# Twelve-stage transformer kernel: in the first two attentions the output projection of the first token tile is issued behind the last six units; sparse attention's output projection takes its k tiles in another order

## What is computed

```python
na0:  neighbourhood attention, 16 heads of 64, position bias     (touched)
ffn0: silu(h @ Wg) * (h @ Wu) @ Wd, inner width 2816
dil0: dilated attention, 16 heads, three projections per head    (touched)
ffn1, ffn2
rwrt: two recurrent mixers side by side, then @ ev_w_out
xa0:  attention over a memory of 256 tokens, 4 heads
ffn3, ffn4
dsa:  sparse attention (top 64 of the keys for each token) for 8 heads,
      beside a short convolution over 512 channels;
      concat([o, conv]) @ od_w_out                               (touched)
xa1:  attention over the memory again (mem_norm @ wk, @ wv)      (its memory load is touched)
ffn5
```

## Time and profile before

| | |
|---|---|
| time of three runs | 2300.5, 2303.89, 2302.1 us; median 2302.1 us |
| profiled execution | 2304.5 us, its span 2302.7 us |
| busy | TensorE 92%, weight loads 85%, VectorE 62%, ScalarE 41% |
| TensorE's granted clock, mean | 0.947 of 2.4 GHz |

### The profile page before, as it was taken

One profiled execution on the slowest core, in us unless ns is written; L12 is line 12 of the kernel. 1 busy time (PEld: TensorE's weight loads), 2 busy tenths in 40 slices (PEclk: granted clock), 3 DMA queues, 4 the chain that ended last, 5 costly groups with the idle time before them and its releaser, 6 DMA issues.

```text
span 2302.7 us, 37011 instructions
## 1 busy us (share of the span) xinstructions
PE 2117.8 (92%) x14998; PEld 1948.3 (85%) x14998; DVE 1427.3 (62%) x1925; ACT 935.2 (41%) x1225; POOL 27.4 (1%) x46
## 2 busy tenths in 40 slices
PE   7989999999999999999955988999999996689998
PEld 6769989998879989998944977899899895588997
DVE  5747746665647756765677546576577455565773
ACT  4534434344444434444311324444444342444442
POOL 0000000000000000000000000000000000000000
PEclk9989999999999999999976978899999997898999
DMA  7325554443415554555520024255455551142553
GB/s 279 130 82 183 193 199 170 151 147 114 162 47 184 195 196 152 195 192 184 199 76 9 1 80 149 94 189 193 158 188 188 202 182 73 51 162 89 192 192 110
DMA packets 49789, 341.47 MB, mean 148 GB/s; under 512 B 5776, under 2 KB 6544, under 8 KB 9616
## 3 DMA queue, kind: packets, MB, share of 16 engines
q1 hardware_dynamic: 45216, 321.21, 38.6%
q10 hardware_dynamic: 4464, 18.68, 2.2%
HBM read 338.82 MB, written 1.05 MB: 148 GB/s over the span
## 4 chain that ended last, share of the span: by engine, by line
PE 81%; DVE 13%; ACT 3%; issue 2%; DMA 0%; POOL 0%; DVEq 0%; ACTq 0%; SPq 0%; POOLq 0%
PE pj L226 14%; PE pj L227 14%; PE pj L228 14%; PE acc L232 7%; PE acc L234 7%; PE acc L233 7%; DVE wlo L302 2%; PE pj L560 2%; PE acc L628 2%; PE pj L232 2%; PE pj L234 2%; PE pj L233 2%; PE pj L566 1%; ACT whi L295 1%; PE acc L616 1%
## 5 line engine op out<-in xcount | busy, mean ns | idle before, releaser
L302 DVE TENSOR_TENSOR wlo<-raw,whi 128x2048 fp32r<-128x2048 f32 x288 | 659.8, 2291 | 346.7 <-ACT whi L295 345.8
L226 PE MATMUL pj<-xh,whi 128*128 128x256 f32 x2704 | 771.1, 285 | 18.1 <-DVE wlo L312 13.2
L227 PE MATMUL pj<-xl,whi 128*128 128x256 f32 x2704 | 767.8, 284 | 0.0
L228 PE MATMUL pj<-xh,wlo 128*128 128x256 f32 x2704 | 767.7, 284 | 0.0
L295 ACT ACTIVATE whi<-raw 128x2048 fp32r<-128x2048 f32 x299 | 569.6, 1910 | 475.2 <-PE acc L234 240.8
L226 PEld LDWEIGHTS pj<-xh,whi 128*128 128x128 f32 x2704 | 521.9, 193 | 21.2 <-issue 15.7
L227 PEld LDWEIGHTS pj<-xl,whi 128*128 128x128 f32 x2704 | 522.0, 193 | 0.0
L228 PEld LDWEIGHTS pj<-xh,wlo 128*128 128x128 f32 x2704 | 521.8, 193 | 0.0
L232 PE MATMUL acc<-whi,AR 128*128 128x512 f32 x688 | 275.6, 401 | 9.5 <-DVE AR L1875 4.4
L233 PE MATMUL acc<-whi,AR 128*128 128x512 f32 x688 | 274.3, 399 | 0.0
L234 PE MATMUL acc<-wlo,AR 128*128 128x512 f32 x688 | 274.1, 398 | 0.0
(11 more groups left out here) (351 smaller groups left out, 2421.4 us busy)
## 6 DMA issues: line engine op xcount, KB each, us to landing
raw<-in_wstream SPq DMA_DIRECT2D x302, 1024.0 KB, 4.8
F<-in_gains ACTq DMA_DIRECT2D x12, 512.0 KB, 5.4
F<-in_rpb ACTq DMA_DIRECT2D x3, 1024.0 KB, 4.8
F<-in_memtok ACTq DMA_DIRECT2D x2, 1024.0 KB, 4.8
F<-in_memin ACTq DMA_DIRECT2D x2, 1024.0 KB, 6.9
F<-in_small ACTq DMA_DIRECT2D x1, 1536.0 KB, 10.6
F<-in_xin SPq DMA_DIRECT2D x2, 512.0 KB, 6.5
xt<-in_xtok SPq DMA_DIRECT2D x1, 1024.0 KB, 11.9
```

Source lines behind the costliest of these rows:

```text
L226: nc.tensor.matmul(o, wh, k_hi, start=first, stop=False, skip_group_check=True)
L227: nc.tensor.matmul(o, wh, k_lo, start=False, stop=False, skip_group_check=True)
L228: return nc.tensor.matmul(o, wl, k_hi, start=False, stop=last, skip_group_check=True)
L302: nc.vector.tensor_tensor(wlo[:, gs, :], raw[:, gs, :], whi[:, gs, :].bitcast(F32), ALU.subtract).then_inc(w_lo, 1)
```

## The change

`na0` and `dil0`: for i = 10 to 15 `fill(i)` ends in `first_half(i - 10)`, which issues the six 512-column matmuls of the first token tile (both column halves) for k tile i - 10, into `pj[0]` and `pj[1]`. They take the place of the filler matmuls of i = 12 to 15. `out_pe` leaves those products out of its first three chunks and does the rest: 12 matmuls in each of these chunks, 24 in the last. `post_act` and `post_dve` read the first token tile from `pj[0]`, `pj[1]`.

`dsa`: the weights' rows and the k tiles are taken in the order 4, 5, 6, 7, 0, 1, 2, 3, so the convolution's tiles come first; `out_pe` no longer waits for all eight tiles; the `UV` product goes behind the first chunk and into `pj[0]`, `pj[1]`. ACT rounds the convolution's tiles and issues the memory's loads ahead of the attention, and squares the memory right behind it; the memory's transposed copy gets another place in SBUF for this stage.

```diff
@@ -407,23 +407,27 @@
             nc.vector.tensor_scalar(ss[:, 8:10], ss[:, 4:6], 1.0 / D, EPS, ALU.mult, ALU.add)\
                 .then_inc(sg(tag, "mv"), 1)
-        def post_act(act, w, tag):
+        def out_banks(kind):
+
+            return [pj[0], pj[1], acc[2], acc[3]] if kind in ("na", "dil") else acc
+
+        def post_act(act, w, tag, ob):
             for b in range(4):
                 if b < 3:
                     act.wait_ge(*at(tag, "ob", b + 1))
                 else:
                     act.wait_ge(w_used, w.g + 1)
-                nc.scalar.activation(JUNK[:, b * 512:(b + 1) * 512], acc[b][:, :], ACT.Square, accum_out=ss[:, b:b + 1])\
+                nc.scalar.activation(JUNK[:, b * 512:(b + 1) * 512], ob[b][:, :], ACT.Square, accum_out=ss[:, b:b + 1])\
                     .then_inc(sg(tag, "sq"), 1)
             act_phase(act, w, 1)
-        def post_dve(dve, w, tag, half, nxt):
+        def post_dve(dve, w, tag, half, nxt, ob):
             tmp = [Sb[:, 0, :], Sb[:, 1, :], PTb[:, 0, :], PTb[:, 1, :]]
             def scaled(b):
                 dve.wait_ge(*at(tag, "sq", b + 1))
-                link(dve, nc.vector.scalar_tensor_tensor(tmp[b], acc[b][:, :], half * D ** 0.5,
+                link(dve, nc.vector.scalar_tensor_tensor(tmp[b], ob[b][:, :], half * D ** 0.5,
                                                          GB[:, (b % 2) * 512:(b % 2 + 1) * 512], ALU.mult, ALU.mult))
             def mean(t):
@@ -472,7 +476,8 @@
             for _ in range({3: 2, 4: 2, 5: 0}[n]):
                 nc.tensor.matmul(mb[:, T:2 * T], ident, cst[:, 0:T], start=True, stop=True)
-        def out_pe(pe, w, nk, lo_at, tag, ready, nxt, beside=lambda pe, c: None, fill=keep_busy, kt0=0):
+        def out_pe(pe, w, nk, lo_at, tag, ready, nxt, beside=lambda pe, c: None, fill=keep_busy, kt0=0,
+                   ob=acc, early=0):
             post = tag + "post"
             def last_chunk(g):
@@ -483,7 +488,7 @@
                     t, h = divmod(b, 2)
                     for kk in range(2):
                         wk = slice(kk * D + h * 512, kk * D + (h + 1) * 512)
-                        x = mm3t(acc[b][:, :], whi[:, gs, wk], wlo[:, gs, wk], AR[:, k0 + kk, t * P:(t + 1) * P],
+                        x = mm3t(ob[b][:, :], whi[:, gs, wk], wlo[:, gs, wk], AR[:, k0 + kk, t * P:(t + 1) * P],
                                  AR[:, lo_at + k0 + kk, t * P:(t + 1) * P], False, kk == 1)
                     if b == 3:
                         x.then_inc(w_used, 1)
@@ -509,12 +514,12 @@
                 pe.wait_ge(w_lo, g + 1)
                 for kk in range(2):
                     pe.wait_ge(*at(tag, ready, c * 2 + kk + 1))
-                    for b in range(4):
+                    for b in range(2 if c < early else 0, 4):
                         t, h = divmod(b, 2)
                         tt = slice(t * P, (t + 1) * P)
                         kt = (2 * c + kk + kt0) % nk
                         wk = slice(kk * D + h * 512, kk * D + (h + 1) * 512)
-                        x = mm3t(acc[b][:, :], whi[:, gs, wk], wlo[:, gs, wk], AR[:, kt, tt],
+                        x = mm3t(ob[b][:, :], whi[:, gs, wk], wlo[:, gs, wk], AR[:, kt, tt],
                                  AR[:, lo_at + kt, tt], c == 0 and kk == 0, False)
                 x.then_inc(w_used, 1)
                 beside(pe, c)
@@ -806,7 +811,8 @@
         mem_hi, mem_lo = AR[:, 16:24, :], AR[:, 24:32, :]
-        mem_raw = F0[:, 32 * T:40 * T].rearrange("p (k t) -> p k t", t=T)
+        raw_at = {mt_: F0[:, a:a + 8 * T].rearrange("p (k t) -> p k t", t=T)
+                  for mt_, a in (("s6m", 32 * T), ("s10m", 8984))}
         mem_tok = F0[:, 24 * T:32 * T].rearrange("p (t n) -> p t n", n=D)
         mem_rs = mn[:, 0:2]
@@ -837,14 +843,14 @@
             return fill
         def mem_act(act, mt, c):
-            if c == 0:
+            if c == (-1 if mt == "s10m" else 0):
                 act.wait_ge(*at(mt, "ld", 32))
                 for t in range(2):
                     nc.scalar.activation(JUNK[:, t * D:(t + 1) * D], mem_tok[:, t, :], ACT.Square,
                                          accum_out=mn[:, 2 + t:3 + t]).then_inc(sg(mt, "sq"), 1)
             if c == 1:
                 for k in range(KT):
-                    nc.scalar.activation(mem_hi[:, k, :], mem_raw[:, k, :], ACT.Copy, scale=v("mem_g", k))\
+                    nc.scalar.activation(mem_hi[:, k, :], raw_at[mt][:, k, :], ACT.Copy, scale=v("mem_g", k))\
                         .then_inc(sg(mt, "hi"), 1)
         def mem_dve(dve, mt, c):
...
@@ -983,13 +989,23 @@
                             w.g += 1
                             w.p += 1
                         done[0] += 1
-                    if i >= 3 * UP:
-                        for _ in range(3 if na else 5):
-                            nc.tensor.matmul(pj[0][:, 0:T], ident, cst[:, 0:T], start=True, stop=True)
+                    if i >= 10:
+                        first_half(i - 10)
+
+                def first_half(kt):
+
+                    c, kk = divmod(kt, 2)
+                    gs = (w.g + c) % 3
+                    pe.wait_ge(w_lo, w.g + c + 1)
+                    pe.wait_ge(*at(tag, "od", kt + 1))
+                    for h in range(2):
+                        wk = slice(kk * D + h * 512, kk * D + (h + 1) * 512)
+                        mm3t(pj[h][:, :], whi[:, gs, wk], wlo[:, gs, wk], AR[:, kt, 0:P], AR[:, 8 + kt, 0:P],
+                             kt == 0, False)
                 attn_pe(pe, tag, units, 0, deep=1, fill=fill)
                 pe.wait_ge(*at(tag, "od", 8))
-                out_pe(pe, w, 8, 8, tag, "od", nxt)
+                out_pe(pe, w, 8, 8, tag, "od", nxt, ob=out_banks(kind), early=3)
             def bias_pass(dve, ps_):
@@ -1243,15 +1259,18 @@
                 pe.wait_ge(S("qlc"), 4)
                 pe.wait_ge(S("mask"), 1)
                 attn_pe(pe, tag, units, 0)
-                pe.wait_ge(*at(tag, "od", DH))
-                for h in range(DH):
-                    rows = slice(64 * (h % 2), 64 * (h % 2) + 64)
-                    last = nc.tensor.matmul(acc[h // 4][rows, (h // 2 % 2) * T:(h // 2 % 2 + 1) * T],
-                                            UV[:, h * 64:(h + 1) * 64], OL[:, h, :], start=True, stop=True)
-                last.then_inc(S("o"), 1)
-                pe.wait_ge(S("rdy"), 8)
-                out_pe(pe, w, 8, 8, tag, "rdy", nxt, lambda pe, c: mem_pe(pe, nmt, c),
-                       first_keys(w, nmt))
+
+                def between(pe, c):
+                    if c == 0:
+                        pe.wait_ge(*at(tag, "od", DH))
+                        for h in range(DH):
+                            rows = slice(64 * (h % 2), 64 * (h % 2) + 64)
+                            last = nc.tensor.matmul(pj[h // 4][rows, (h // 2 % 2) * T:(h // 2 % 2 + 1) * T],
+                                                    UV[:, h * 64:(h + 1) * 64], OL[:, h, :], start=True, stop=True)
+                        last.then_inc(S("o"), 1)
+                    mem_pe(pe, nmt, c)
+
+                out_pe(pe, w, 8, 8, tag, "rdy", nxt, between, first_keys(w, nmt), 4)
             def dve_f(dve, w):
                 for c in range(9):
@@ -1320,7 +1339,7 @@
                 for k in range(8):
                     kt = (k + 4) % 8
                     dve.wait_ge(S("oh"), k + 1 if k < 4 else 8)
-                    src = hb[:, kt - 4, :] if kt >= 4 else acc[kt // 2][:, (kt % 2) * T:(kt % 2 + 1) * T]
+                    src = hb[:, kt - 4, :] if kt >= 4 else pj[kt // 2][:, (kt % 2) * T:(kt % 2 + 1) * T]
                     nc.vector.tensor_tensor(AR[:, 8 + kt, :], src, AR[:, kt, :].bitcast(F32), ALU.subtract)\
                         .then_inc(S("rdy"), 1)
                 out_dve(dve, w, 8, lambda dve, c: mem_dve(dve, nmt, c))
@@ -1351,17 +1370,18 @@
                 def fin(grp):
                     nc.scalar.activation(OL[:, 2 * grp:2 * grp + 2, :].rearrange("p a t -> p (a t)"),
                                          o_pair(grp)[:, :], ACT.Copy).then_inc(sg(tag, "od"), 2)
-                attn_act(act, tag, units, 0, fin)
                 act.wait_ge(S("cv"), 4)
                 for k in range(4):
                     nc.scalar.activation(AR[:, 4 + k, :], hb[:, k, :], ACT.Copy).then_inc(S("oh"), 1)
+                mem_load(act, nmt)
+                attn_act(act, tag, units, 0, fin)
+                mem_act(act, nmt, -1)
                 act.wait_ge(S("o"), 1)
                 for k in range(4):
-                    nc.scalar.activation(AR[:, k, :], acc[k // 2][:, (k % 2) * T:(k % 2 + 1) * T], ACT.Copy)\
+                    nc.scalar.activation(AR[:, k, :], pj[k // 2][:, (k % 2) * T:(k % 2 + 1) * T], ACT.Copy)\
                         .then_inc(S("oh"), 1)
                 act.wait_ge(S("rdy"), 8)
-                mem_load(act, nmt)
-                out_act(act, w, s, 8, lambda act, c: mem_act(act, nmt, c))
```

(11 more changed lines are left out.)

## The result

The changed kernel takes 2278.7 us at the median of four runs (2277.9 to 2281.2), beside 2301.4 us for the kernel before: a ratio of 0.9902, 95% interval 0.9884 to 0.9919, or 22.7 us less. The forecast was 2276.9 us, a ratio of 0.9891. The profiled execution took 2278.9 us, its span is 2277.1 us.

The account below looks back on a forecast made before the run. TensorE, busy 92% of the span, was taken as the bound: what it issues plus its waits. `na0` 9.6, `dil0` 10.4 and `dsa` 5.2 sum to 25.2 us, so 2302.1 - 25.2 = 2276.9 us, range 2269 to 2288.

Parts of the forecast that it names:

- Part 1: Projections of `na0` and `dil0`: 36 of 96 matmuls leave at 0.234 us each, 8.4 us per attention; weights' margin 1.2 us.
- Part 2: `na0` tail: moved groups close gaps, full clock returns earlier, 1.2 us gained; `na0` in all 9.6 us, bounds 7.0 to 10.7.
- rival 1: Attention tails: clock stays low longer, 2.6 us in `na0` and 1.1 in `dil0` lost, 2280.6 us; chance 0.14.
- Part 3: `dil0` tail: groups fill a wait, avoid a clock fall (1.1 us) and replace longer fillers; 2.0 us earlier.
- Part 4: `dsa`, last values to broadcast: projection chunks fill TensorE's idle stretches, clock penalty goes; 5.2 us, bounds 3.6 to 5.5.
- Rival 2: Attention projections become bound by their weights; in the extreme 8.4 us come back in both, 2293.7 us; chance 0.06.
- Rival 3: `dsa` gives its gain back before the next stage, through work queued on ACT; 2282.1 us; chance 0.05.
- Rival 4: Attentions slower: clock stays at 1.2 GHz from 118 us to the projection's end, 14.2 us per attention, 2325 us; chance 0.03.

Follow-up runs that it names:

- Experiment 6: Changed kernel with three of four products (nine matmuls) in each group, the third in `pj[2]`: 2277.7 us, ratio 0.9906.
- after: The changed kernel itself, against the kernel before: 2278.7 us at the median of four runs, ratio 0.9902.
- only_na_dil: Changed kernel with the parts for `dsa` taken back, so only the two attentions are changed: 2282.1 us, ratio 0.9912.
- mem_load_old: Changed kernel with the memory's loads and squares back behind ACT's wait for all eight tiles: 2282.4 us, ratio 0.9917.
- experiment 4: Changed kernel with the six groups later: two behind unit 12, two behind 13, one each behind 14 and 15: 2287.4 us, ratio 0.9937.
- experiment 5: Same run as `mem_load_old`: changed kernel with the memory's loads and squares back behind ACT's wait for all eight tiles: 2282.4 us, ratio 0.9917.
- second timing: Changed kernel, unedited, timed again with more runs of the kernel before: 2277.1 us, ratio 0.9888.
- experiment 8: Changed kernel with two groups behind unit 9, one each behind 11, 12, 13 and 15, none behind 10 and 14: 2279.8 us, ratio 0.9904.

## Why the prediction was right

**Part 1, the projection.** The forecast was right to 0.02 us in both attentions, and so was the claim on which it stands: the last chunk's weights were there 1.2 us ahead. Experiment 6 took the margin away and got the wait of the size that the same sum gives. The price per matmul from the traced block, 0.234 us, held; by the Trainium skill's 131 ns ("TensorE: Matmul & The Clock Gate", section "Back-to-back issue gap") the two projections would have gained 72 x 0.131 = 9.4 us, an estimate, and they gained 16.8.

**Part 2, the tail of `na0`.** The mechanism is shown: groups close the gaps, the clock is back by 123 us instead of 131. The size, 1.2 us, is one of several: the traces of after gave 1.54, 0.57 and 0.28 (22.65, 23.62 and 23.91 against 24.19), `only_na_dil` 0.13 and `mem_load_old`, with the same code up to there, 1.53 (22.66). The unit with a group takes 3.40 us, not 3.20: 0.2 us pass around a group that the sum left out. Those two units and the end of the tail cost 0.6 us more than forecast; in the traces of after and `mem_load_old` the first unit was 0.9 us shorter than forecast (4.9 us, 5.84 forecast), because the clock came back within it, and in the three others it took 5.89 to 6.11 us. So the first trace lands near 1.2 because two misses nearly cancel, and that is luck; the mean of the five is 0.8. The three with the late clock are a part of rival 1, at most 1.1 of its 2.6 us, and within the bounds of the step.

**Part 3, the tail of `dil0`.** 2.0 us forecast, 2.03 measured, and within 0.2 in the other traces. The groups lie mostly in DVE's time, the fall at 634 to 640 is gone in every trace with groups from unit 10 on, and the last values start behind a group of 1.4 us instead of fillers of 2.35. The price of the fall, 1.1 us, is less sure than the rest: experiment 4 has no fall there either, with TensorE waiting as in the kernel before, so that the groups removed it is likely and not shown.

**Part 4, `dsa`.** 5.2 us forecast, 5.21 measured. The loads that I costed at nothing were rightly hidden, by ACT's wait for the selection. What they cost uncovered I named too small: I wrote that they would stand in ACT's square and not in the projection, and experiment 5 shows TensorE waiting 3.35 us in the projection for what hangs on the square.

**The rivals.** Rival 2 does not hold here and begins one product further on. Rival 3 did not happen: 1979.47 to 1992.65 is without a wait, and from this broadcast to the next one, at the start of `xa1`, it is 24.19 us where it was 23.97. Rival 4 did not: the clock is at 1.00 behind 124 us. The difference between 25.2 forecast and 22.7 first measured is inside the interval (18.6 to 26.7); with the second timing it is 24.7.

## What to carry to other kernels

Work that waits only for parts that are long finished can leave a block that is on the path and go into the gaps ahead of it, and its worth is the number of instructions that leave, at the spacing of that same block, as long as the gaps have room for them and what the block itself hides (here the next weights) keeps its margin. Work that margin out first, it says how much can be moved; beyond it, or beyond the room in the gaps, the gain stops (experiment 6). Place matters as much as amount: two groups in the one long idle stretch and none in front of the last values gave another 5 to 7 us for the same work. And when an order is changed so that an engine no longer waits, look at what used to be hidden in that wait; here a load had to be moved with it.

## What the runs showed of the hardware

TensorE's clock does not fall and rise at the same place in two executions of one program. In three traces of the changed kernel the tail of `na0` took 22.65, 23.62 and 23.91 us, and the start of `dil0` differed in clock (0.72 and 0.88 from 425 to 435 us), and `dsa`'s selection (0.84, 0.84 and 0.67 over 20 us, worth 3.3 us), with the same instructions. That moves a run of this kernel by some microseconds either way (after ran at 2272.9 to 2281.2 us in nine executions), about as much as the smaller terms of the sum, so those are read from stretches of a trace and not from the total. The length of one idle stretch does not tell whether a fall follows. In experiment 8 one followed a wait of 1.67 us in `na0` and none a wait of 2.34 us in `dil0`; and the waits of 0.92 and 1.80 us in `dil0`'s tail were followed by a fall in the kernel before (0.72 from 634 to 640 us) and by none in experiment 4 (1.00).
